# Value projections of two models in slots of 512 rows by 512 columns, with matmuls 512 wide

## The reference

```
mixer (2 layers): dv = (u @ w_in)[..., dv columns]        # 1024 x 512
    a = softmax(map 0) - lam * softmax(map 1);  o = a @ dv
even layer:       v = (h @ even_w_in)[..., v columns]     # 1024 x 1024, 8 heads of 128
    w[t,s] = exp(log_beta + rest), s < t;  o = w @ v, then * silu(z_a)
odd layer:        v = (h @ odd_w_in)[..., v columns]      # 1024 x 1024, 4 heads of 256
    state = exp(g_last) * state + k_dec^T v;  o = scores @ v + q_dec @ state; rms_norm(o) * silu(z)
```

## Time and profile before

| what | us |
|---|---|
| median of three runs | 1508.74 |
| lowest, highest | 1508.28, 1511.12 |
| the profiled execution: its own time | 1506.61 |
| its span, first to last instruction | 1504.6 |
| PE busy | 1490.0 (99%) |
| PE weight loads busy | 1383.0 (92%) |
| DVE busy | 1188.2 (79%) |
| ACT busy | 795.2 (53%) |
| mean DMA rate | 173 GB/s |

### The profile page before, as it was taken

The page is one execution under the profiler, slowest core; times in us unless marked ns, Lnnn a source line. Parts: engine busy times, 40 slices in busy tenths (PEclk is TensorE's granted clock), DMA queues, the critical chain, the costliest instruction groups (busy, mean ns, idle before and its releaser), DMA issues.

```text
span 1504.6 us, 25373 instructions
## 1 busy us (share of the span) xinstructions
PE 1490.0 (99%) x10802; PEld 1383.0 (92%) x10802; DVE 1188.2 (79%) x1567; ACT 795.2 (53%) x1010; POOL 44.5 (3%) x43
## 2 busy tenths in 40 slices
PE   7999999999999999999999999999999999999999
PEld 6888899999988888888899999999999999999989
DVE  7987777797898865988668678888998899766744
ACT  6444456565554443544446466455535645775653
POOL 0000001210000000000001110000000000000000
PEclk9999999999999999999999999999999999999999
DMA  7555445434555545455544443455554453325531
GB/s 284 200 194 194 172 161 188 150 141 144 191 183 192 196 172 204 184 196 195 183 164 160 180 151 141 159 223 188 200 188 180 158 195 137 117 105 190 184 125 57
DMA packets 38687, 260.50 MB, mean 173 GB/s; under 512 B 4656, under 2 KB 5040, under 8 KB 9136
## 3 DMA queue, kind: packets, MB, share of 16 engines
q1 hardware_dynamic: 37856, 257.84, 47.4%
q10 hardware_dynamic: 720, 1.05, 0.2%
HBM read 257.83 MB, written 1.05 MB: 172 GB/s over the span
## 4 chain that ended last, share of the span: by engine, by line
PE 93%; DVE 5%; ACT 1%; issue 0%; DMA 0%; ACTq 0%
PE ps L260 22%; PE ps L209 14%; PE ps L211 13%; PE ps L210 13%; PE ps L262 11%; PE ps L681 8%; PE ps L683 4%; DVE w_low L199 2%; PE ps L1400 1%; PE ps L1391 0%; PE ps L1380 0%; ACT w_high L192 0%; DMA w_raw<-in_weights 0%; DVE scratch L2072 0%; PE ps L1415 0%
## 5 line engine op out<-in xcount | busy, mean ns | idle before, releaser
L192 ACT ACTIVATE w_high<-w_raw 128x2048 fp32r<-128x2048 f32 (+3 forms) x244 | 458.5, 1880 | 407.8 <-PE ps L211 182.3
L199 DVE TENSOR_TENSOR w_low<-w_raw,w_high 128x2048 fp32r<-128x2048 f32 (+3 forms) x244 | 551.1, 2261 | 116.3 <-ACT w_high L192 114.1
L260 PE MATMUL ps<-x,w_high 128*128 128x512 f32 x1408 | 494.9, 396 | 9.4 <-DVE w_low L811 9.4
L262 PE MATMUL ps<-x,w_low 128*128 128x256 f32 x1408 | 393.6, 280 | 0.0
L260 PEld LDWEIGHTS ps<-x,w_high 128*128 128x128 f32 x1408 | 265.3, 188 | 70.9 <-issue 9.3
L262 PEld LDWEIGHTS ps<-x,w_low 128*128 128x128 f32 x1408 | 266.6, 189 | 0.1
L209 PE MATMUL ps<-x,w_high 128*128 128x256 f32 (+1 forms) x904 | 260.9, 289 | 0.5 <-DVE x L296 0.2
L211 PE MATMUL ps<-x,w_low 128*128 128x256 f32 (+1 forms) x904 | 255.7, 283 | 0.0
L210 PE MATMUL ps<-x,w_high 128*128 128x256 f32 (+1 forms) x904 | 255.6, 283 | 0.0
L681 PE MATMUL ps<-ffn_hid,w_high 128*128 128x512 f32 x528 | 183.2, 390 | 0.0
L209 PEld LDWEIGHTS ps<-x,w_high 128*128 128x128 f32 (+1 forms) x904 | 172.6, 191 | 5.5 <-issue 4.6
(11 more groups left out here) (451 smaller groups left out, 2370.0 us busy)
## 6 DMA issues: line engine op xcount, KB each, us to landing
w_raw<-in_weights SPq DMA_DIRECT2D x229, 1024.0 KB, 4.8
w_raw<-in_weights SPq DMA_DIRECT2D x10, 768.0 KB, 4.2
w_raw<-in_weights SPq DMA_DIRECT2D x5, 512.0 KB, 3.8
even_second_vectors<-in_second SPq DMA_DIRECT2D x1, 1836.0 KB, 8.2
w_raw<-in_weights SPq DMA_DIRECT2D x2, 640.0 KB, 3.9
resid<-in_x SPq DMA_DIRECT2D x4, 256.0 KB, 6.1
w_raw<-in_weights ACTq DMA_DIRECT2D x4, 256.0 KB, 7.6
out<-resid SPq DMA_DIRECT2D x3, 256.0 KB, 2.4
```

Source lines behind the costliest of these rows:

```text
L192: act.activation(self.wh[:, j, 0:SIZES[n]], self.raw[:, j, 0:SIZES[n]], ACT.Copy).then_inc(self.hi_made, 1)
L199: dve.tensor_tensor(self.wl[:, j, 0:SIZES[n]], self.raw[:, j, 0:SIZES[n]], self.wh[:, j, 0:SIZES[n]].bitcast(F32), ALU.subtract).then_inc( ...
L260: pe.matmul(c.bank(bank + i).rearrange("p (a t) -> p a t", a=2), wh[:, k, f], c.x[:, :, k, :], start=(k == 0), stop=False, skip_group_chec ...
L262: mm = pe.matmul(c.bank(bank + i, SEQ), wl[:, k, f], c.xh[:, k, :], start=False, stop=(k == DT - 1), skip_group_check=True)
```

## The change

Value slots come in pairs: each slot of a pair holds 512 rows (4 row tiles) of the same 512 columns, and the pair fills two banks, one for each half of the tokens, each 512 columns wide. The first slot starts both banks, the second completes them. The number of slots and of bytes stays. In the even layer the values of pairs 0 and 1 are now taken after slot 18 and that of pair 2 after slot 19, with a third buffer for weights and another output bank for pair 1. In the odd layer `own_states(2)` moves into the middle of slot 9.

```diff
+def values_half(c, pe, banks, n, half, between=None):
+    wh, wl = c.weights_at(n, DT // 2, 2 * FC)
+    pe.wait_ge(c.lo_made, c.made(n))
+    for i, bank in enumerate(banks):
+        if i and between:
+            between()
+        t = slice(i * P, (i + 1) * P)
+        for k in range(DT // 2):
+            at = half * DT // 2 + k
+            mm = exact3(pe, c.bank(bank), c.xh[:, at, t], c.xl[:, at, t], wh[:, k, :], wl[:, k, :], half == 0 and k == 0,
+                        half == 1 and k == DT // 2 - 1)
+        if half:
+            mm.then_inc(c.done, 1)
+    if not half:
+        mm.then_inc(c.done, 1)
...
# mixer, ACT and PE
-                for i in range(2):
-                    ins = act.activation(m.dv[:, i, FC * (n - S_DV):FC * (n - S_DV) + FC], c.halves(bank)[:, i, :],
-                                         ACT.Copy, scale=c.scale_column(i))
+                ins = act.activation(m.dv[:, part, :], c.bank(bank), ACT.Copy, scale=c.scale_column(part))
-            plain(S_DK + a)
+            (half_slot if S_DV <= S_DK + a < S_POOL else plain)(S_DK + a)
...
# even layer
-A_ATT, A_SUFFIX, A_PV = 14, 15, 17
+A_ATT, A_SUFFIX = 14, 15
+A_PV = {18: (0, 1), 19: (2,)}
+        return self.c.halves({1: even_unit(A_V + 1) % 3, PAIRS - 1: 6}.get(p, 5))
# ACT: weights
-            if p >= 2:
-                act.wait_ge(self.pv_made, p - 1)
-            act.activation(e.w[p % 2], self.score_banks(p), ACT.Exp).then_inc(self.w_made, 1)
+            if p == 2:
+                act.wait_ge(self.q_wide, QK_SLOTS)
+            if p == 3:
+                act.wait_ge(self.pv_made, 1)
+            act.activation(e.w[p], self.score_banks(p), ACT.Exp).then_inc(self.w_made, 1)
# ACT: values, in the loop over n
-            if n >= A_V:
+            if n >= A_V and (n - A_V) % 2:
+                value(n - 1)
                 value(n)
# PE: values(p)
-            pe.wait_ge(self.read_a, even_emptied(even_unit(A_V + p)))
+            pe.wait_ge(self.read_a, even_emptied(even_unit(A_V + 2 * (p // 2) + 1)))
-            if 0 < p < PAIRS - 1:
-                pe.wait_ge(self.oa_made, p)
+            if p == 2:
+                pe.wait_ge(self.oa_made, 1)
-            if n >= A_PV:
-                values(n - A_PV)
+            for p in A_PV.get(n, ()):
+                values(p)
...
# odd layer, PE
-            pe.wait_ge(self.read_a, odd_emptied(G_V + h))
+            pe.wait_ge(self.read_a, odd_emptied(G_V + 2 * (h // 2) + 1))
-                project(c, pe, b, base + n, DT, tokens=G_V <= n < G_Z,
-                        midway=(lambda: self.norm.mean(pe)) if n == 1 else None).then_inc(c.done, 1)
+                project(c, pe, b, base + n, DT,
+                        midway={1: lambda: self.norm.mean(pe), 9: lambda: own_states(2)}.get(n)).then_inc(c.done, 1)
             if n == 8:
-                own_states(2)
                 output(0)
```

More of the change, by code:

```diff
@@ L67 @@
 APART_FILLS = [1] * (2 * FF_STEPS) + [2 if m in FF_ENDS and m < LAST else 1 for m in range(FF_STEPS)]
[L68 to L70 removed]
+MIX_FILLS = [{S_UQ: 3, S_UKV: 4, S_DV + 1: 2}.get(n, 2 if S_BRANCH <= n < S_OUT else 1) for n in range(MIX_SLOTS)]
+EVEN_FILLS = [2 if n in (A_V + 1, A_V + 3, A_GLU) else 1 for n in range(EVEN_SLOTS)]
+ODD_FILLS = [2 if n in (G_V + 1, G_V + 3, ODD_SLOTS - 1) else 1 for n in range(ODD_SLOTS)]
 FF_UNITS, MIX_UNITS = sum(FF_FILLS), sum(MIX_FILLS)
@@ L860 @@
          + [(S_UKV, p, "act") for p in range(4)] + [(n, 0, "dve") for n in range(S_DK, S_DV)]
-         + [(n, 0, "act") for n in range(S_DV, S_POOL)] + [(n, 0, "dve") for n in range(S_POOL, S_BRANCH)]
+         + [(S_DV, 0, None), (S_DV + 1, 0, "act"), (S_DV + 1, 1, "act")] + [(n, 0, "dve") for n in range(S_POOL, S_BRANCH)]
          + [(n, p, "dve") for n in range(S_BRANCH, S_OUT) for p in range(2)]
@@ L870 @@
 FIRST_KV, FIRST_PAIRED, FIRST_BRANCH = unit_of(S_UKV), unit_of(S_DK), unit_of(S_BRANCH)
+HALF_VALUES = unit_of(S_DV)
 def unit_bank(u):
@@ L1356, in plain, with half_slot @@
             b = bank_free(u)
-            project(c, pe, b, base + n, DT, norm=norm, tokens=S_DV <= n < S_POOL, midway=midway).then_inc(c.done, 1)
+            project(c, pe, b, base + n, DT, norm=norm, midway=midway).then_inc(c.done, 1)
+        def half_slot(n):
+            half, units = n - S_DV, [unit_of(S_DV + 1, i) for i in range(2)]
+            values_half(c, pe, (unit_bank(u) if half else bank_free(u) for u in units), base + n, half)
         def kv_slot():
@@ L1873, in filled @@
     def filled(self, u):
-        return self.c.done, self.units + u + 1
+        halves = sum(u >= even_unit(n) for n in (A_V, A_V + 2))
+        return self.c.done, self.units + u + halves + 1
     def emptied(self, u):
@@ L1913, in value @@
         def value(n):
-            u = even_unit(n)
+            u, four, i = even_unit(n), (n - A_V) // 2, (n - A_V) % 2
             act.wait_ge(*self.filled(u))
[L1916 to L1919, removed]
+            act.activation(e.v[:, i, 2 * FC * four:2 * FC * four + 2 * FC], c.bank(u % 3), ACT.Copy,
+                           scale=c.scale_column(i)).then_inc(self.read_a, 1)
         def rows(j):
@@ L2011, in scalar @@
                 silu(n)
-            if n >= A_PV:
-                attention_high(n - A_PV)
+            for p in A_PV.get(n, ()):
+                attention_high(p)
         glu_gate(0)
@@ L2136, in vector @@
                 normalised(n - A_Q)
-            if n >= A_PV:
-                gated(n - A_PV)
+            for p in A_PV.get(n, ()):
+                gated(p)
             if 0 <= n - A_ATT < PAIRS:
@@ L2146, in vector @@
                 scan(A_S5.index(n))
-            if n >= A_PV:
-                attention_low(n - A_PV)
+            for p in A_PV.get(n, ()):
+                attention_low(p)
             if n == A_V - 1:
@@ L2279, in tensor @@
         for n in range(A_GLU):
-            b = bank_free(even_unit(n))
             j = n - A_Q - 2
-            project(c, pe, b, base + n, DT, norm=None if n else self.norm, tokens=n >= A_Q,
-                    midway=(lambda: spread(j)) if 0 <= j < QK_SLOTS else None).then_inc(c.done, 1)
+            if n >= A_V:
+                half = (n - A_V) % 2
+                values_half(c, pe, (even_unit(m) % 3 if half else bank_free(even_unit(m)) for m in (n - half, n - half + 1)),
+                            base + n, half, (lambda: spread(j)) if j < QK_SLOTS else None)
+            else:
+                project(c, pe, bank_free(even_unit(n)), base + n, DT, norm=None if n else self.norm, tokens=n >= A_Q,
+                        midway=(lambda: spread(j)) if 0 <= j < QK_SLOTS else None).then_inc(c.done, 1)
             if n == 1:
@@ L2364, in filled, with filled_values @@
         return self.c.done, FILLED[self.base + n]
+    def filled_values(self, two, i):
+        return self.c.done, FILLED[self.base + G_V + 2 * two + 1] - 1 + i
     def emptied(self, n):
@@ L2399, in evac @@
         def evac(n):
[L2400 to L2404, removed]
+            two, i = (n - G_V) // 2, (n - G_V) % 2
+            act.wait_ge(*self.filled_values(two, i))
+            act.activation(o.v[:, i, 2 * FC * two:2 * FC * two + 2 * FC], c.bank(odd_bank(n)), ACT.Copy,
+                           scale=c.scale_column(i)).then_inc(self.read_a, 1)
         def silu(n):
@@ L2452, in scalar @@
                 part_high(1)
-            if G_V <= n < G_Z:
+            if G_V <= n < G_Z and (n - G_V) % 2:
+                evac(n - 1)
                 evac(n)
@@ L2688, in tensor @@
         for n in range(G_OUT):
-            b = bank_free(n)
-            if n == G_R:
+            if G_V <= n < G_Z:
+                second = (n - G_V) % 2
+                values_half(c, pe, (odd_bank(m) if second else bank_free(m) for m in (n - second, n - second + 1)),
+                            base + n, second)
+            else:
+                b = bank_free(n)
+            if G_V <= n < G_Z:
+                pass
+            elif n == G_R:
                 wh, wl = c.weights_at(base + n, DT, P)
@@ L2954, in even_slots @@
                                                       (D, 2 * D, 3 * D, 4 * D, 4 * D + S5_W, 4 * D + 2 * S5_W)))
-    return slots([tiles(x, FC) for x in (u, zb, za, q, k, v)] + [tiles(w_glu, S5_W), tiles(w_out, P)])
+    return slots([tiles(x, FC) for x in (u, zb, za, q, k)] + [half_tiles(v, 2 * FC), tiles(w_glu, S5_W), tiles(w_out, P)])
 def pack_second(a):
@@ L2992, in odd_slots @@
     wide[:, 0:GLA_RANK] = r
-    return slots([tiles(wide, P)] + [tiles(x, FC) for x in (q, k, v, z)] + [tiles(w_out, FC)])
+    return slots([tiles(wide, P)] + [tiles(q, FC), tiles(k, FC), half_tiles(v, 2 * FC), tiles(z, FC)] + [tiles(w_out, FC)])
 def laid_out(a):
```

21 lines of the change are left out of this document (15 added, 6 removed).

## The result

| | before | after |
|---|---|---|
| median of 14 runs each, us | 1508.75 | 1512.53 |
| lowest, highest | 1506.79, 1511.50 | 1509.69, 1514.07 |
| the profiled execution, its span | 1506.61, 1504.6 | 1514.07, 1512.3 |
| mean granted clock of that execution | 1.000 | 0.999 |

The ratio is 1.0022 with an interval of 1.0014 to 1.0029: 3.3 us slower (2.1 to 4.4). The forecast was 1508.9 with a range to 1511.8, so it was wrong, on the side of rival A.

What follows compares the result with a forecast made beforehand. PE's own pace was taken to bound the kernel, busy 1490.0 of 1504.6 us. Terms -2.9 + 2.85 + 0.1 + 0.1 = +0.15 us gave a median of 1508.9, range 1507.0 to 1511.8 for 8 in 10.

Steps and rivals of the forecast that it cites:

- rival A: Even layer: the clock falls in the stall at values(2), PE then runs slower; 1510.3 to 1511.8 us, chance 0.28.
- Pace: Value slots of six pairs: 288 wide matmuls each save 10 ns over two narrow ones, 2.9 us in all.
- Rival C: Value slots: long streams of wide matmuls run at 0.2375 us, only 0.7 us saved; 1511.1 us, chance 0.06.
- The wait: Even layer, behind slot 19: PE stalls 2.85 us at values(2) for ACT's split and two copies, nothing hiding it.
- rival B: Even layer: ACT's copies come ahead of values(2), so there is no stall; 1506.0 us, chance 0.07.
- ACT's share: Value-slot copies: one wide copy replaces two, ACT gains some tenths of a us a slot, worth nothing by itself.
- mid-slot waits: First slot of each pair: second bank needed half a slot after the first, 2.5 us of room; no cost taken.
- suffixes(3): Even layer: PE reaches it 1.28 us sooner, scores' logs for pair 3 come about as early as needed; 0 taken.
- rival D: A mid-slot wait or the chain to turn(0) costs 1 to 2 us more; 1510 to 1511 us, chance 0.12.
- turn(0): Odd layer: moving own_states(2) into slot 9 tightens ACT's chain to it; stall of 0.1 us (0 to 0.4).
- -2.9 + 2.85 + 0.1 + 0.1 = +0.15: Whole kernel: matmul gain, even-layer stall, cutting slot 9 in two and the stall at turn(0), in us.
- a fall that comes during the wait costs less: Even-layer stall: argument against the clock fall costing its full 2.8 us, or 1.4 for half the low-clock time.

Runs made afterwards that it cites:

- e2: Kernel before, all slots narrow, with only the change's wait of values(2) for slot 19's copies: 1513.88 us, 1.0028 against before.
- e3: Changed kernel with twelve unused 512-column matmuls keeping PE at work in the wait ahead of values(2): 1508.77 us, 0.9995 against before.
- e7: Changed kernel with ACT's two copies of values ahead of split_high(22): 1510.95 us, 0.9994 against before.
- e5: Changed kernel, unedited, timed again beside the kernel before: 1512.65 us, 1.0005 against before.
- e10: Kernel before with the change made in the even layer alone: 1513.82 us, 1.0027 against before.
- e8: Changed kernel with PE's glu(0) put ahead of values(2), second measurement of that edit: 1508.39 us, 0.9981 against before.
- e9: Changed kernel with glu(0) ahead of values(2) and DVE's split_low(22) ahead of gated(2): 1506.32 us, 0.9973 against before.
- e6: Kernel before with the change made in the mixers and odd layer, not the even layer: 1510.87 us, 0.9991 against before.
- e1: Kernel before, unedited, timed again beside itself: 1510.80 us, 1.0003.

## Why the prediction was wrong

*Pace: mechanism right, size a little short.* Forecast: 10 ns a wide matmul, 2.9 us in all, with 2.0 to 3.7 as bounds. Measured: 0.57 us in each mixer, 0.38 + 0.58 in the even layer (slots 16 and 17, then the pair of 18 and 19, where a slot takes 5.55 us and took 5.84), 1.12 in the odd layer: 3.2 us, or 11 ns each. Six matmuls in a row of before had given the pace of 288. Rival C, and the rule of the Trainium skill that gave the same quarter of the gain ("TensorE: Matmul & The Clock Gate", "Back-to-back issue gap", where it is meant for a matmul by itself), are out: the odd pair's 0.227 us against twice 0.120 is five times the 2.5 ns that it allows.

*The wait: right.* Forecast 2.85 us with ACT's split and two copies in it, counted from where the next matmul would have started; so counted it was 3.0, and 2.83 of idle time by the trace (in e2 2.87 and 2.71 with narrow copies, which are 0.81 us for two). That `values(2)` has nothing to hide it was right, and so was that nothing later pays it back. That the wait "is written out" and would not be covered was right (rival B out). The forecast gave ACT 0.2 us to see the end of the slot, 1.38 for the split and 1.2 to 1.3 for the copies; the rows give 0.26, 1.39 and 1.34 up to PE's start.

*ACT's share, mid-slot waits, `suffixes(3)`: right.* PE has no other new wait in its view (rival D out). *`turn(0)`: a tenth too much.* No wait, against 0.1 forecast.

*The failed step: the sum took the cost of the stall as its length.* "-2.9 + 2.85 + 0.1 + 0.1 = +0.15" has no term for what PE does after the stall. The clock fell behind it in 10 of 14 executions and cost 1.64 us in the profiled one. With that term, the measured gain and the measured wait the sum is -3.2 + 3.0 + 1.6 = +1.4, the +1.46 us of the stage times. The mechanism was named, and its price was bounded well (1.4 to 2.8 us, for 3 or 6 us at the low clock, which lasted 3.41), but it got 0.28 where it held most of the chance. Two things were there to be weighed more. The only idle time of like length in the trace of before, after the last matmul, did end with the clock going down. And "a fall that comes during the wait costs less" was argued as a comfort, while the earlier trace rows put the fall some 2.5 us after the last matmul's end, where a stall of 2.83 us is nearly over, so that almost the whole spell meets a busy engine. In the four profiled stalls the fall came later still, 3.6 to 4.2 us after the end of the last matmul, with PE at work again. e3 shows that the fall hangs on PE's idleness and not on waiting as such: the same wait with PE at work cost no clock. The Trainium skill's warning in the same page ("Why this matters for your kernels"), that idle gaps between bursts send the engine back to its low clock, came out here for gaps of 2.7 and 2.8 us, in 32 of 46 executions, and not for the 1.28 us of e7; the page speaks of somewhat longer gaps, and the runs decide.

*The rest of the distance.* The profiles explain +1.5 us, the first measurement says +3.3 (2.1 to 4.4), the second +0.8 (-0.6 to 2.3). With +1.5 the time would have been 1510.2, inside the range of 1507.0 to 1511.8: the missing term moved the forecast by 1.6 us, and what took the time out of the range is this unexplained rest of 1.8. What lies between was not tied to any instruction of the change. The feed-forward paces of the next section move single executions by 2.3 us a stage, and the median of before alone was 1508.75, 1510.26, 1512.18 and 1510.81 us in four sets of runs. That chance in these paces made the difference between the two measurements is the likely reading, but only the profiled executions show a pace, so it is argued and not shown. Nor is it shown that the program has no part in which pace comes.

## What to carry to other kernels

On an engine that is 99% busy, a hole costs its length and then what the clock does after it: put both into the sum before calling a change even. When a merge of two buffers makes a consumer wait for the later one, look for independent work of the hole's length to put ahead of the consumer (here `glu(0)`, which turned +1.5 us into -2.8 by the stage times), and take whatever the consumer doesn't need out from in front of its producer. Where runs of one program spread over 6 us (those of before did), compare the touched stages from landmark to landmark in the traces, since these repeat to some hundredths of a microsecond.

## What the runs showed of the hardware

**The clock came down after the stall, not in it.** In the four profiled executions with a stall of 2.7 or 2.8 us the granted clock was still 1.00 when PE resumed, and fell 0.97 us later in after, 0.81 in e5, 1.04 in e2 and 1.40 in e10; each time it stayed at 0.50 for 3.41 us with PE busy throughout. After the last matmul there is a further idle time, of 3.3 to 3.4 us in all twelve traces. In nine of them the clock came down within it, as in before (0.84 over the last 2.6 us); in after, e8 and e9 it did not. This is after's:

```profile
1509.60:1512.30 2.70, 0.00 (x0) 0.00 (x0) 0.00 (x0) 0.00 (x0) 0.00 (x0) 1.00 0.14 49
```

So the clock can be down before an idle time of this length is over, and need not be.

**One stream of matmuls has two paces.** The second to fourth feed-forward, whose own instructions nothing touches, came out close to one of two totals in every profiled execution, and not the same one in each stage: first to last wide matmul 122.1 or 124.4 us in the second and third stage (about 231.5 or 236.4 ns from a wide matmul to the next start), and 175.4 or 176.9 us in the fourth, 175.4 in e6 and e10 alone, the two kernels with a part of the change. Before had 122.12 and 122.12 in the two, e1, the same program, 124.44 and 122.14; after 124.45 and 124.37; e9 122.12 and 124.37. The granted clock was 1.00 throughout and the order of work on each engine is the written one. What chooses the pace was not found, and a part of the program in it is not ruled out (see behind the table of stages).
